# Turning x inside the first unit of a hybrid decoder block, with extra unit-matrix products on TensorE

## What is computed

```
h = jnp.concatenate([meta, x], axis=1)                  # 16 + 512 tokens, 2048 channels
y = xf * lax.rsqrt(jnp.mean(xf * xf, axis=-1, keepdims=True) + RMS_EPS)
hn = y * w                                              # rms_norm(h, norm_mix_w)
proj = hn @ w_in
q, k, v, z, b_logit, a_logit, p, gate_a, gate_b = jnp.split(proj, split_idx, axis=-1)
...                                                     # delta rule, pooling, merge, out, FFN, final norm
```

## Time and profile before

| | us |
|---|---|
| median of 3 runs | 2724.19 |
| lowest and highest run | 2724.11, 2726.44 |
| span of the profiled execution, first to last instruction | 2722.7 |
| own time of the profiled execution | not listed beside the runs |
| PE busy in it | 2651.1 (97%) |

### The profile page before, as it was taken

One profiled execution on the slowest core, in us unless ns is written; L12 is line 12 of the kernel. 1 busy time (PEld: TensorE's weight loads), 2 busy tenths in 40 slices (PEclk: granted clock), 3 DMA queues, 4 the chain that ended last, 5 costly groups with the idle time before them and its releaser, 6 DMA issues.

```text
span 2722.7 us, 44448 instructions
## 1 busy us (share of the span) xinstructions
PE 2651.1 (97%) x17640; PEld 2422.1 (89%) x17640; DVE 1835.8 (67%) x1771; ACT 998.4 (37%) x1025; POOL 341.3 (13%) x350
## 2 busy tenths in 40 slices
PE   8999999999999999998989999999999998999997
PEld 8999988888889987887879999999999996888885
DVE  4444555555553234558888888888888887888886
ACT  4443322222222242223354444444444543333333
POOL 5000044444442420110000000000000000000000
PEclk9999999999999999999999999999999999999998
DMA  4333222223223433778425444545445449756661
GB/s 139 98 92 92 79 78 78 77 77 85 77 77 93 108 93 122 254 241 306 165 97 170 155 150 146 177 152 161 154 154 177 146 141 316 227 194 214 220 213 62
DMA packets 345654, 398.73 MB, mean 146 GB/s; under 512 B 11481, under 2 KB 300386, under 8 KB 344418
## 3 DMA queue, kind: packets, MB, share of 16 engines
q1 hardware_dynamic: 286514, 334.34, 39.1%
q10 hardware_dynamic: 59072, 63.44, 6.8%
HBM read 325.92 MB, written 71.83 MB: 146 GB/s over the span
## 4 chain that ended last, share of the span: by engine, by line
PE 92%; DVE 3%; issue 2%; DMA 1%; ACT 1%; POOL 0%; SPq 0%; DVEq 0%; ACTq 0%; POOLq 0%
PE psum L1973 34%; PE psum L2285 10%; PE psum L2283 10%; PE psum L2284 10%; PE psum L2260 6%; PE psum L2261 6%; PE psum L2262 6%; PE psum L2133 2%; PE psum L2128 1%; PE psum L1922 1%; PE psum L1950 1%; DMA w_raw<-in_w_proj_a 1%; PE psum L2112 1%; PE psum L2205 1%; DVE hq L1630 0%
## 5 line engine op out<-in xcount | busy, mean ns | idle before, releaser
L1973 PE MATMUL psum<-hn_hi,w_hi 128*128 128x264 f32 (+1 forms) x1600 | 450.4, 330 | 0.0
L1973 PE MATMUL psum<-hn_hi,w_lo 128*128 128x264 f32 (+1 forms) x1600 | 449.6, 330 | 0.0
L1973 PE MATMUL psum<-hn_lo,w_hi 128*128 128x264 f32 (+1 forms) x1600 | 449.4, 330 | 0.0
L1296 DVE TENSOR_TENSOR w_lo<-w_raw,w_hi 128x1024 fp32r<-128x1024 f32 x144 | 186.9, 1299 | 253.8 <-ACT w_hi L892 253.4
L1973 PEld LDWEIGHTS psum<-hn_lo,w_hi 128*128 128x128 f32 x1600 | 269.0, 188 | 22.7 <-issue 0.7
L1973 PEld LDWEIGHTS psum<-hn_hi,w_lo 128*128 128x128 f32 x1600 | 268.6, 188 | 22.5
L1973 PEld LDWEIGHTS psum<-hn_hi,w_hi 128*128 128x128 f32 x1600 | 269.0, 188 | 22.0 <-issue 0.2
L892 ACT ACTIVATE w_hi<-w_raw 128x1024 fp32r<-128x1024 f32 x144 | 152.0, 1057 | 371.9 <-PE psum L1973 345.5
L2260 PE MATMUL psum<-dn_hi,act_hl 128*128 128x512 f32 x616 | 242.3, 393 | 15.8 <-DVE hq L1630 14.6
L2261 PE MATMUL psum<-dn_lo,act_hl 128*128 128x512 f32 x616 | 241.5, 392 | 0.0
L2262 PE MATMUL psum<-dn_hi,act_hl 128*128 128x512 f32 x616 | 241.3, 392 | 0.0
(11 more groups left out here) (352 smaller groups left out, 6318.1 us busy)
## 6 DMA issues: line engine op xcount, KB each, us to landing
w_raw<-in_w_in SPq DMA_DIRECT2D x144, 512.0 KB, 3.9
ffn_raw<-in_w_ffn_gate SPq DMA_DIRECT2D x44, 1024.0 KB, 6.4
ffn_raw<-in_w_ffn_up SPq DMA_DIRECT2D x44, 1024.0 KB, 6.5
dn_raw<-in_w_ffn_down SPq DMA_DIRECT2D x40, 1024.0 KB, 7.3
act_hl<-act_dram SPq DMA_DIRECT2D x70, 512.0 KB, 9.3
act_dram<-comb_hi ACTq DMA_DIRECT2D x22, 896.0 KB, 4.2
act_dram<-comb_lo ACTq DMA_DIRECT2D x22, 896.0 KB, 6.2
out_raw<-in_w_out SPq DMA_DIRECT2D x16, 1024.0 KB, 9.7
```

The costliest lines, as they stand in the source:

```text
L1296: dve.tensor_tensor(wlo[s][:], raw[s][:], whi[s][:].bitcast(F32), ALU.subtract).then_inc(S["lo_ready"], 1)
L1973: ins = pe.matmul(o, lhs, r, start=kt == 0 and i == 0, stop=kt == 4 * n_chunks - 1 and i == 2)
```

## The change

Four things are changed, all ahead of the end of pass 0 of the first unit.

- PE turns only tiles 0, 1 and 2 ahead of the first unit. Tile 3 is turned after chunk 0 of pass 0 and tile 4 after chunk 1.
- ACT squares tiles 3 and 4 after the high halves of tile 2, between its halves of chunks 0 and 1 and after chunk 1. The chunks 2 and 3 follow tiles 3 and 4.
- DVE and POOL follow that order: DVE makes the diagonal of tile 3 between chunks 0 and 1 and that of tile 4 ahead of tile 3's quads; POOL makes 1/rms of tiles 3 and 4 after the low halves of tile 2.
- PE gets products of the 128 x 128 unit matrix with itself, into bank 3, which nobody reads: 18 ahead of its wait for the parameter rows, and one after each quad of tile 0.

```diff
@@ gpsimd
             for u in range(TT + 1):
-                if 3 <= u + 2 <= TT:
-                    rms_of_x(u + 2)
+                if u == 3:
+                    rms_of_x(3)
+                    rms_of_x(4)
                 lo_quads(u, xy, x_tokens(u), META if u == 0 else P)
@@ scalar
             for u in range(TT + 1):
-                if 3 <= u + 2 <= TT:
-                    square_tile(u + 2)
                 hi_quads(u, xy, x_tokens(u), META if u == 0 else P)
-                if u >= 2:
-                    split(u - 2, u - 2)
-            split(SLOTS - 1, SLOTS - 1)
+                if u == 2:
+                    split(0, 0)
+                    square_tile(3)
+                    split(1, 1)
+                    square_tile(4)
+                if u >= 3:
+                    split(u - 1, u - 1)
@@ vector
             for u in range(TT + 1):
-                if 2 <= u + 1 <= TT:
-                    diagonal(u + 1)
+                if u == 1:
+                    diagonal(2)
                 weight_quads(u, xy, nmix, x_tokens(u), META if u == 0 else P)
-                if u >= 2:
-                    split(u - 2, u - 2)
-            split(SLOTS - 1, SLOTS - 1)
+                if u == 2:
+                    split(0, 0)
+                    diagonal(3)
+                    split(1, 1)
+                if u == 3:
+                    diagonal(4)
+                if u >= 3:
+                    split(u - 1, u - 1)
@@ tensor
+            def keep_running(n):
+
+                for _ in range(n):
+                    pe.matmul(PS[:, 3, 0:P], ident[:], ident[:], start=True, stop=True)
+
             def turn_quads(u, src, rows):
...
                     ins.then_inc(S["x_turned"], 1)
+                    if u == 0:
+                        keep_running(1)
...
             pe.wait_ge(S["consts_built"], 2)
+            keep_running(18)
             pe.wait_ge(S["rows_landed"], 80)
...
             turn_quads(0, x_cols(0), META)
-            for t in range(TT - 1):
-                turn_quads(t + 1, x_cols(t + 1), P)
+            for u in range(1, 3):
+                turn_quads(u, x_cols(u), P)
...
             first_unit(G_A, hn_halves, half_banks, "a_done", (2, TT),
-                       lambda c: turn_quads(TT, x_cols(TT), P) if c == 0 else None, ab_products)
+                       lambda c: turn_quads(c + 3, x_cols(c + 3), P) if c < 2 else None, ab_products)
```

## The result

| | us |
|---|---|
| after, median of 6 runs (lowest to highest) | 2735.84 (2731.62 to 2741.96) |
| before, 6 runs beside them | 2725.14 (2720.29 to 2727.42) |
| ratio after / before, 95% interval | 1.0043 (1.003 to 1.0056) |
| the profiled execution of after, and its span | 2736.91, 2735.0 |

The change makes the kernel slower by about 11 us. The forecast was 2722.7 us with a range up to 2726.4: wrong in sign and far outside the range. The two profiled executions differ by 2735.0 - 2722.7 = 12.3 us of span, about the difference of the medians, so they are a fair pair in which to look for it.

The account below looks back on a forecast made before the run. PE, busy 97% of the 2722.7 us span, bounds the kernel. First product 5.2 us earlier, less 3.6 (tile 3), less 0.3 (slow clock), plus 1.33 less 1.3 (waits): about 1.5 us gained, 2722.7 us, range 2720.2 to 2726.4.

Parts of the forecast that it names:

- The part on the 18 products: PE ahead of the parameter rows: 36 slow instructions, 7.7 us, ending at 9.4 at the latest, delaying the rows 0.4 us.
- The change touches nothing later: After the first unit: PE runs on unbroken, so only its end of that unit, now 69.2 us, matters.
- The last rival: After the first unit: a later wait ending at a fixed time swallows the change, 2724.2 us; chance 4%.
- The products raise the clock ahead of tile 0: PE's start: the unit products bring the fast clock by 9.3 us; rows turned from 8.7.
- Tile 0 at 0.11 us an instruction: PE's turning of tile 0: 40 instructions at the fast clock, 4.4 us, done at 13.7 instead of 15.8.
- the second rival: Tile 0: the clock is lost, some 4 us at half pace, first product at 28.1, 2724.7 us; chance 27%.
- DVE's chain of 8.7 us from tile 1's last quad to the first product: DVE before chunk 0: 8.9 us less 0.2 for the moved diagonal, so the first product comes at 26.1.
- Chunk 0 slow after the pause: Pass 0, chunk 0: PE's idle time lowers the clock, losing 2.0 us, so it takes 4.9 us, to 31.0.
- Tile 3 on the path, tile 4, and the wait ahead of chunk 3: PE in pass 0: 3.6 us for each tile, then a 1.3 us wait for chunk 3's low half.
- The logits and pass 1 unchanged: End of the first unit: both take as long as before, with pass 1 ending near 67.7 us.
- The other engines cost nothing: ACT, POOL and DVE in pass 0: diagonal ready about 30.4, PE's tile 3 quads first at 31.9; no cost.
- the term for tile 3: Pass 0 between chunks 0 and 1: turning this tile there costs PE 3.6 us, formerly hidden behind DVE.

Follow-up runs that it names:

- 76: The kernel before plus 76 PE instructions of already met semaphore waits ahead of the parameter rows, no unit products: 2738.54 us, ratio 1.0053.
- 70: The kernel before plus 70 PE instructions of already met semaphore waits ahead of the parameter rows, no unit products: 2725.65 us, ratio 1.001.

## Why the prediction was wrong

**The term that was missing.** The part on the 18 products costs them as 36 instructions of 0.213 us and as nothing else, and the four in tile 0 are costed the same way. All 22 together also make PE's program 87 instructions longer, and that cost 4.5 + 4.3 + 2.5 = 11.3 of the 12.3 us. The step that failed is the sentence "The change touches nothing later. So the whole question is when PE finishes the first unit". It held for the order of all queues and not for the place of PE's code in its instruction memory. The last rival said of what comes after 70 us that PE is without a break to 286 us; that was right, and the loop that lost the time begins only at about 330. What the prediction named as its breaking point, a wait of PE after 70 us that wasn't there before, is what came.

Could it have been foreseen? The page of before lists the queue q8, and in the loop it made 8 fetches in four rounds, which says that the code stayed in. With the loop's end at 3767 and 256 instructions to a packet, 72 instructions were free until the next line. The Trainium skill ("Advanced Engine Details and Errata", section "ISA Cache") states a line of 16 kB or 256 instructions and 128 kB for TensorE, so eight lines. That should have raised the question. By the letter of that rule a loop over eight lines would still fit; in the runs eight are fetched anew each round (34 fetches) and seven are not (8). The stated size need not be wrong: with one line fetched ahead, as the 9 packets a round suggest, a loop over eight needs nine. The section's remark that there are only two lines doesn't fit TensorE here, where a loop over seven stays in. The measurement decides: here, seven lines are the most that a loop kept.

**Step by step, in the first unit.** The other steps can be read in the chain of after.

- *The products raise the clock ahead of tile 0.* Right, and earlier than I had it: their 36 instructions took 6.60 us from 1.58 on, 0.18 each and not 0.213, and did not come into the rows' way. The rows were turned from 8.11, not at 8.7.
- *Tile 0 at 0.11 us an instruction.* Wrong; here the second rival was the right one (27%). All engines from 9 to 20 us, columns of rows 7:

```profile
9.00:14.00 5.00, 5.00 (x36) 4.56 (x35) 0.78 (x4) 3.05 (x9) 2.05 (x6) 0.93 1.01 421
14.00:17.00 3.00, 3.00 (x14) 2.96 (x15) 1.15 (x5) 0.26 (x1) 0.00 (x0) 0.50 1.03 274
17.00:20.00 3.00, 3.00 (x16) 3.00 (x15) 1.01 (x2) 1.26 (x2) 1.51 (x2) 0.50 1.08 371
```

  The clock was up, was lost at about 13.3 with PE busy throughout, and tile 1 ran at half pace. Before, 24 instructions took these 5 us, now 36, but the following 30 took 6. The rival had taken some 4 us at half pace; it was 6.8, from 13.3 to 20.1. The Trainium skill's rule that I weighed ("TensorE: Matmul & The Clock Gate", section "What's actually happening", a budget of time whatever is issued) would have held the clock up here; the trace is against it, as rows 3 were. Rows 3 should have had more weight than 27%.
- *DVE's chain of 8.7 us from tile 1's last quad to the first product.* Nearly right: DVE took that quad at 21.05 and the product began at 29.27, 8.2 us later. The first product came 2.1 us earlier than before, not 5.2; the rival had 28.1, 3.2 us earlier.
- *Chunk 0 slow after the pause.* Right: PE waited 4.69 us for the low half, and the 24 instructions took 5.17 us (forecast 4.9) at a clock of 0.50.
- *Tile 3 on the path, tile 4, and the wait ahead of chunk 3.* Right in kind and near in size: 3.57, 3.67, and a wait of 0.95 us for `w_lo` up to 48.45 (forecast 3.6, 3.6, 1.3). In the sum the term for tile 3 was sized right, and it is larger than what the early clock gave.
- *The logits and pass 1 unchanged.* Right: 7.74 and 11.55 us.
- *The other engines cost nothing.* Right. DVE stood 0.85 us for POOL's 1/rms ahead of the diagonal of tile 3, beside PE's chunk 0, and the next quads came only after that.

```profile
29.97 0.29 DVE L1304 TENSOR_SCALAR diag<-ident,rms 128x128 f32<-128x128 f32 x1 [0.85 <-POOL rms L714]
...
35.37 0.69 DVE L1312 TENSOR_TENSOR xy<-psum,vec_b 128x512 f32<-128x512 f32 x1 [3.98 <-PE psum L1935]
```

So the sum for the first unit failed by its first term, the clock in tile 0: of 5.2 us only 2.1 came, the other terms together took 3.8, and 1.7 us are lost. In the experiments pass 1 started between 0.1 us earlier (the change with its products in a loop) and 4.3 us later (17 products) than before; none of that reaches the 12.3 us. The forecast of almost no change held for the change as an order of work and failed for it as code. Even there the gain of 1.5 us didn't come: the first product was 3.1 us earlier and not 5.2, and pass 1 started 0.07 us earlier.

None of the versions beats the kernel before.

## What to carry to other kernels

Instructions that are added ahead of a long loop body move its code, and a loop that fits the instruction memory with little to spare can stop fitting, far from the edit. So count the lines of 256 instructions that each large loop touches before and after an edit, compare the instruction queue's packets in the loop's stretch, and take a wait named "issue" at a loop's return as a sign of it. Filler and repeated work is better written as a loop: here the 18 products took 7.15 us in a loop against 6.60 written out, and the program grew by 24 instructions instead of 87.

## What the runs showed of the hardware

**Code that no longer fits.** A loop of PE over seven lines of 256 instructions was fetched once (6 packets of 16 kB in the first of four rounds, none in the others, 2 at the way out); over eight it was fetched in each round (9 packets in each of the last three), with waits of 2.0 to 2.7 us at each return. Six instructions more or fewer, 76 against 70, decided over 12.9 us. The pieces of waiting in after, 2.52 + 2.29 + 2.01 = 6.8 us, are only some 60% of the 11.3 us: behind two of the three returns the clock was at 0.50 for another 3 us, and these returns cost 2 us more than their waits. That isn't the same in every kernel: with the products alone the clock fell behind all three returns, with 19 products behind the first alone (0.50 from 470 to 476 us, 1.00 in 607 to 610 and 743 to 746).

**The clock falls under a busy engine.** In seven kernels with the unit products ahead of tile 0 (after and all with such products but the one with 17) it was up when tile 0 began and fell to 0.50 between 12 and 14 us, in the one with 36 products at some 15 us, with PE busy without a pause since tile 0's start, while tile 0's products of 16 columns and the unit products among them ran. Three products of 128 columns after each quad, 12 in all, didn't prevent it. With 13 products ahead of the rows and then 1.52 us of idleness it was at 0.50 from 8.9 us on, to 22.5. Why the clock falls there is open; no experiment settled it.
